# A hybrid retention and sparse-attention block: two projection chunks side by side, wider modulation sums, a re-cut last stage

## The reference, cut to what matters

```python
mod = silu(c) @ w_ada + b_ada                       # six vectors of 1024
sh1, sc1, ga1, sh2, sc2, ga2 = split(mod, 6)
h = rmsnorm(x, ln_mix_g) * (1 + sc1) + sh1
(rq, rk, rv, rg, nq, nkc, nvc, nks, nvs, nkw, nvw, ngate) = split(h @ w_in)   # 2840 columns
y_ret = retention(rope(rq), rope(rk) * RET_DK ** -0.5, rv) * silu(rg)
# three attention branches: compressed blocks, selected blocks, sliding window
y_nsa = nsa(rope(nq), nkc, nvc, rope(nks), nvs, rope(nkw), nvw, ngate, ...)
x = x + ga1 * (concat([y_ret, y_nsa]) @ w_out)
h2 = rmsnorm(x, ln_ffn_g) * (1 + sc2) + sh2
x = x + ga2 * ((silu(h2 @ w_ff_gate) * (h2 @ w_ff_up)) @ w_ff_down)
return rmsnorm(x, ln_final_g)
```

## Time and profile before

| | us |
|---|---|
| median of 3 runs | 727.98 |
| the profiled execution, device time | 729.54 |
| its span, first to last instruction | 727.70 |
| TensorE busy | 682.1 (94%) |
| VectorE busy | 332.8 (46%) |
| GpSimd busy | 265.9 (37%) |
| ScalarE busy | 225.5 (31%) |
| mean granted clock of TensorE | 0.976 of full |

### The profile page before, as it was taken

The page is one execution under the profiler, slowest core; times in us unless marked ns, Lnnn a source line. Parts: engine busy times, 40 slices in busy tenths (PEclk is TensorE's granted clock), DMA queues, the critical chain, the costliest instruction groups (busy, mean ns, idle before and its releaser), DMA issues.

```text
span 727.7 us, 9019 instructions
## 1 busy us (share of the span) xinstructions
PE 682.1 (94%) x3547; PEld 564.1 (78%) x3547; DVE 332.8 (46%) x587; ACT 225.5 (31%) x378; POOL 265.9 (37%) x127
## 2 busy tenths in 40 slices
PE   2678899999989898999999999999999999999995
PEld 1556679987768687888898888888888888888884
DVE  4878999977465668152620110000000029633126
ACT  4435233422132333332542222222222213232222
POOL 2316443432000111138034434434434427545531
PEclk9699999999998899999999999999999999999999
DMA  9975986665000000176014233233233223232002
GB/s 314 359 257 152 353 293 234 199 240 228 30 2 1 0 2 1 40 221 202 1 48 127 87 96 107 87 98 104 87 102 101 89 86 117 86 103 72 0 1 116
DMA packets 73962, 88.09 MB, mean 121 GB/s; under 512 B 3048, under 2 KB 57536, under 8 KB 73792
## 3 DMA queue, kind: packets, MB, share of 16 engines
q1 hardware_dynamic: 73184, 86.36, 36.0%
q0 software_dynamic: 416, 1.08, 0.4%
q10 hardware_dynamic: 320, 0.07, 0.0%
HBM read 85.41 MB, written 2.10 MB: 120 GB/s over the span
## 4 chain that ended last, share of the span: by engine, by line
PE 78%; DVE 10%; ACT 3%; issue 3%; DMA 3%; SPq 2%; POOL 0%; POOLq 0%; DVEq 0%
PE ps L1523 11%; PE ps L1524 11%; PE ps L1522 11%; PE ps L1141 11%; PE ps L1143 11%; PE ps L1142 11%; PE ps L1274 3%; DMA raw<-in_w_in 3%; DVE acc L732 2%; DVE ps L875 1%; SPq L344 1%; PE ps L1332 1%; PE ps L1399 1%; PE ps L1228 1%; ACT hf L488 1%
## 5 line engine op out<-in xcount | busy, mean ns | idle before, releaser
L404 POOL TENSOR_TENSOR wl<-raw,wh 128x1024 fp32r<-128x1024 f32 (+1 forms) x94 | 238.6, 2543 | 285.8 <-ACT wh L456 285.6
L456 ACT ACTIVATE wh<-raw 128x1024 fp32r<-128x1024 f32 (+1 forms) x94 | 97.4, 1039 | 154.4 <-PE ps L1524 73.9
L1522 PE MATMUL ps<-hTh,wh 128*128 128x512 f32 (+1 forms) x384 | 142.8, 372 | 0.0
L1523 PE MATMUL ps<-hTl,wh 128*128 128x512 f32 (+1 forms) x384 | 142.6, 371 | 0.0
L1524 PE MATMUL ps<-hTh,wl 128*128 128x512 f32 (+1 forms) x384 | 142.6, 371 | 0.0
L1106 DVE TENSOR_TENSOR act<-ps,sg 128x512 f32<-128x512 f32 x22 | 15.2, 692 | 212.3 <-PE ps L1524 212.3
L1141 PE MATMUL ps<-wh,hTh 128*128 128x512 f32 (+1 forms) x224 | 90.5, 404 | 11.8 <-DVE hTl L770 10.6
L1143 PE MATMUL ps<-wh,hTl 128*128 128x512 f32 (+1 forms) x224 | 85.8, 383 | 0.0
L1142 PE MATMUL ps<-wl,hTh 128*128 128x512 f32 (+1 forms) x224 | 85.7, 383 | 0.0
L1522 PEld LDWEIGHTS ps<-hTh,wh 128*128 128x128 f32 x384 | 72.4, 188 | 12.5
L1523 PEld LDWEIGHTS ps<-hTl,wh 128*128 128x128 f32 x384 | 72.4, 188 | 12.4
(11 more groups left out here) (197 smaller groups left out, 818.4 us busy)
## 6 DMA issues: line engine op xcount, KB each, us to landing
raw<-in_w_ada SPq DMA_DIRECT2D x32, 512.0 KB, 5.8
raw<-in_w_ff_gate SPq DMA_DIRECT2D x22, 512.0 KB, 3.8
raw<-in_w_ff_up SPq DMA_DIRECT2D x22, 512.0 KB, 3.7
raw<-in_w_ff_down SPq DMA_DIRECT2D x22, 512.0 KB, 3.2
raw<-in_w_in SPq DMA_DIRECT2D x20, 512.0 KB, 7.0
early<-in_w_ada SPq DMA_DIRECT2D x16, 512.0 KB, 9.6
raw<-in_w_out SPq DMA_DIRECT2D x8, 512.0 KB, 6.6
xs<-in_x SPq DMA_DIRECT2D x4, 512.0 KB, 5.3
```

The costliest lines, as they stand in the source:

```text
L404: pool.tensor_tensor(lo, raw[:, slot, 0:n], hi.bitcast(F32), ALU.subtract).then_inc(w_lo, 1)
L456: a.activation(split(u, n)[0], raw[:, slot, 0:n], ACT.Copy).then_inc(w_hi, 1)
L1522: mm(o, hi[:, ks], hTh[:, k, c0:c1], start=k == 0, stop=False)
L1523: mm(o, hi[:, ks], hTl[:, k, c0:c1], start=False, stop=False)
```

## The change

1. The chunks K_CMP and K_WIN run together: units 0, 2, 4, 6 are K_CMP's, units 1, 3, 5, 7 K_WIN's, both over the same quarter of the normed input. K_WIN's outputs lie in banks 4, 5 and 6 and, for the fourth tile, in two pieces in the free ends of banks 4 and 5. Its keys go through the same rotation as the selected keys (four heads at once).
2. ACT's `high` for the first units stands before the transposes' copies and after each pair of blocks, no longer between the two blocks of a pair. Evacuations, transposes, the MLP's waits and the sums for the later modulation vectors get new positions v.
3. `ada_early` treats the two modulation vectors in one instruction, 2 x 256 wide, eight instead of sixteen per quarter.
4. The ring carries five of the six vectors of w_ada until unit 21, the sixth (ga2) during the gate and up projections, where its two row sums follow `gate_up` 11 and 12. The load of the final norm's weights moves behind it.
5. Last stage: the last tile is cut in three pieces, the scaling by the norm's weights goes ahead of the power, DVE finishes one half of a tile and ACT the other, one tile later than before in the streams, and ACT issues the output DMA of its half.

```diff
...
-CHUNKS = [(C_CMP, 512), (C_Q, 512), (C_RQK, 512), (C_WIN, 280), (C_RG, 512), (C_RV, 512)]
-K_CMP, K_Q, K_RQK, K_WIN, K_RG, K_RV = range(6)
+CHUNKS = [(C_CMP, 512), (C_WIN, 280), (C_Q, 512), (C_RQK, 512), (C_RG, 512), (C_RV, 512)]
+K_CMP, K_WIN, K_Q, K_RQK, K_RG, K_RV = range(6)
...
+HALF = D // 2
+PIECES = [[(0, HALF), (HALF, D)]] * (TT - 1) + [[(0, HALF), (HALF, 768), (768, D)]]
...
-AHEAD = 4
+AHEAD = 2
...
-ADA_UNITS = 20
-ADA_OPS = 4 * ADA_START
+ADA_UNITS = 14
+ADA_LAST = 5 * KT
+ADA_FFN = U0_GU + 8
+ADA_OPS = 2 * ADA_START
...
+def chunk_of(u):
+
+    return (u % 2, u // 2) if u < 2 * UPC else divmod(u, UPC)
+
+
 def stream():
 
     items = []
     for q in range(UPC):
-        items += [("early", 4 * q + j) for j in range(4)] + [("w", q)]
+        items += [("early", 4 * q + j) for j in range(4)] + [("w", 2 * q), ("w", 2 * q + 1)]
     a = ADA_START
-    for u in range(3, UNITS):
-        if u > 3:
+    for u in range(2 * UPC - 1, UNITS):
+        if u >= 2 * UPC:
             items.append(("w", u))
-        upto = min(KT * len(ADA), ADA_START - (-(KT * len(ADA) - ADA_START) * (u - 2) // ADA_UNITS))
+        if u < ADA_FFN:
+            upto = min(ADA_LAST, ADA_START - (-(ADA_LAST - ADA_START) * (u - 2 * UPC + 1) // ADA_UNITS))
+        else:
+            upto = min(KT * len(ADA), ADA_LAST + (u - ADA_FFN) // 2 + 1)
         while a < upto:
             items.append(("ada", a))
             a += 1
...
+        def win_out(t):
+
+            if t < TT - 1:
+                return ps[:, 4 + t, 0:P], ps[:, 4 + t, P:280]
+            return ps[:, 4, 280:280 + P], ps[:, 5, 280:432]
...
-                    sp.wait_ge(roped, TT * (K_WIN + 1))
                     sp.dma_start(decay[:, :, :], decays).then_inc(decay_in, 16)
-                if (kind, j) == ("w", U0_GU - 1):
-
+                if (kind, j) == ("w", U0_GU + 34):
                     sp.wait_ge(mod_read, 10)
                     sp.dma_start(gfin[:, :], ln_final_g.partition_broadcast(P)).then_inc(gfin_in, 16)
+                if (kind, j) == ("w", U0_GU - 1):
+
...
-                sp.dma_start(out[t * P:(t + 1) * P, :], xb[:, t % 2, :]).then_inc(out_done[t], 16)
+                sp.dma_start(out[t * P:(t + 1) * P, 0:HALF], xb[:, t % 2, 0:HALF]).then_inc(out_done[t], 16)
             for t in range(TT):
-                sp.wait_ge(out_done[t], 16)
+                sp.wait_ge(out_done[t], 32)
...
-                if u == 3:
+                if u == 2 * UPC:
...
             high(0)
+            high(1)
...
             for k in range(KT):
-                if k % 2 and k < KT - 1:
-                    high(k // 2 + 1)
                 a.wait_ge(mod_read, k // 2 + 1)
...
                 a.activation(hTh[:, k, :], hf[:, k % 2, :], ACT.Copy).then_inc(h_hi, 1)
+                if k % 2 and k < KT - 1:
+                    high(k + 1)
+                    high(k + 2)
...
+                    if ch == K_WIN:
+                        a.wait_ge(unit_used, 2 * UPC)
...
+                    if ch in (K_Q, K_RQK):
+                        a.wait_ge(roped, TT * (ch - 2) + t + 1)
...
             for v in range(U_IN):
-                if v and v % UPC == 0:
-                    evacuate(v // UPC - 1)
-                if v and v + 3 < U_IN:
+                for ch in {7: [K_CMP], 8: [K_WIN], 12: [K_Q], 16: [K_RQK], 20: [K_RG]}.get(v, []):
+                    evacuate(ch)
+                if 2 * UPC <= v + 3 < U_IN:
                     high(v + 3)
-                if 5 <= v <= 8:
-                    pairs_copy(v - 5)
-                for n in {7: [0], 10: [1, 2], 12: [3, 4], 14: [5, 6], 16: [7, 8], 19: [9]}.get(v, []):
+                if 9 <= v <= 12:
+                    pairs_copy(v - 9)
+                for n in {11: [0, 1], 14: [2, 3], 15: [4, 5], 18: [6, 7], 19: [8, 9]}.get(v, []):
...
+            def finish(t):
+
+                a.wait_ge(y_scaled, piece_count(t, len(PIECES[t]) - 1))
+                a.wait_ge(rstd_ok, N_X2 + t)
+                a.activation(xb[:, t % 2, HALF:D], xb[:, t % 2, HALF:D], ACT.Copy, scale=rstd[:, t:t + 1]).then_inc(y_high, 1)
+                a.wait_ge(y_high, t + 1)
+                a.dma_start(out[t * P:(t + 1) * P, HALF:D], xb[:, t % 2, HALF:D]).then_inc(out_done[t], 16)
...
             for t in range(TT):
-                for half in range(2):
-                    a.wait_ge(x2_ok, 2 * t + half + 1)
-                    cols_ = slice(half * 512, (half + 1) * 512)
-                    if t >= 2 and half == 0:
-                        a.wait_ge(out_done[t - 2], 16)
-                    a.activation(xb[:, t % 2, cols_], x1[:, t, cols_], ACT.Square,
-                                 accum_out=(ssq, ssq2)[half][:, t:t + 1]).then_inc(sq3, 1)
+                for n, (c0, c1) in enumerate(PIECES[t]):
+                    a.wait_ge(x2_ok, piece_count(t, n))
+                    if t and n == 0:
+                        a.wait_ge(var_ok, N_X2 + t - 1)
+                    a.activation(sqj[:, c0 % HALF:c0 % HALF + c1 - c0], x1[:, t, c0:c1], ACT.Square, accum_out=part[:, n:n + 1]).then_inc(sq3, 1)
+                    if t and n == 0:
+                        finish(t - 1)
+            finish(TT - 1)
...
-                for o in ops:
-                    p, (kk, i) = 2 * q + o // 8, divmod(o % 8, 2)
-                    j, k = 2 * p + i, 4 * (p % 2) + kk
-                    d.wait_ge(early_in[j % EARLY], 16 * (j // EARLY + 1))
-                    dst = acc[:, i, 2 * q * P:2 * (q + 1) * P]
-                    src = early[:, j % EARLY, 2 * kk * P:2 * (kk + 1) * P]
+                for k in ops:
+                    kh, kk = divmod(k, 4)
+                    j = 4 * q + 2 * kh
+                    for i in range(2):
+                        d.wait_ge(early_in[(j + i) % EARLY], 16 * ((j + i) // EARLY + 1))
+                    dst = acc[:, :, 2 * q * P:2 * (q + 1) * P]
+                    src = early[:, j % EARLY:j % EARLY + 2, 2 * kk * P:2 * (kk + 1) * P]
                     if k == 0:
                         d.tensor_scalar(dst, src, cs[:, k:k + 1], None, ALU.mult).then_inc(ada_used, 1)
                     else:
-                        d.wait_ge(ada_used, 16 * q + o - 1)
+                        d.wait_ge(ada_used, KT * q + k)
                         d.scalar_tensor_tensor(dst, src, cs[:, k:k + 1], dst, ALU.mult, ALU.add).then_inc(ada_used, 1)
...
-            ada_early(0, range(16))
+            ada_early(0, range(KT))
...
                 if q < UPC - 1:
-                    ada_early(q + 1, range(AHEAD, AHEAD + 3))
+                    ada_early(q + 1, range(AHEAD, AHEAD + 2))
                 h_low(2 * q)
                 if q < UPC - 1:
-                    ada_early(q + 1, range(AHEAD + 3, AHEAD + 5))
+                    ada_early(q + 1, range(AHEAD + 2, AHEAD + 3))
                 h_low(2 * q + 1)
                 if q < UPC - 1:
-                    ada_early(q + 1, range(AHEAD + 5, 16))
+                    ada_early(q + 1, range(AHEAD + 3, KT))
...
-                for n in {7: [0], 10: [1, 2], 12: [3, 4], 19: [9]}.get(v, []):
+                for n in {11: [0, 1], 14: [2, 3], 15: [4, 5]}.get(v, []):
...
-                if v == 8:
+                if v == 11:
                     mod_rows(5, ga1, 0)
-                if v == 10:
+                if v == 12:
                     mod_rows(6, ga1, 1)
-                if v == 13:
+                if v == 17:
                     mod_columns(7, 2, 32, 0, KT, 48, 16).then_inc(mod_read, 1)
+                if v == 19:
+                    mod_columns(8, 3, 40, 0, KT, 40, None).then_inc(mod_read, 1)
...
-                if 4 <= v < UPC * (K_WIN + 1) + 2 and v % UPC < 2:
-                    rope_chunk(v // UPC - 1, (0, 1) if v % UPC == 0 else (2, 3))
-                if v == 17:
+                if 2 * UPC <= v < UPC * (K_RQK + 1) + 2 and v % UPC < 2:
+                    rope_chunk(v // UPC - 2, (0, 1) if v % UPC == 0 else (2, 3))
+                if v == 9:
                     d.wait_ge(proj_ev, TT * (K_WIN + 1))
                     d.tensor_scalar(gates[:, :, :], gates[:, :, :], 0.5, 0.5, ALU.mult, ALU.add).then_inc(gates_ok, 1)
                 if v == 18:
-                    mod_columns(8, 3, 40, 0, KT, 40, None).then_inc(mod_read, 1)
                     compressed()
...
+                if f == 12:
+                    mod_rows(9, ga2, 0, bank=4)
+                if f == 13:
+                    mod_rows(10, ga2, 1, bank=5)
                 for u in (U0_GU + 2 * f + 4, U0_GU + 2 * f + 5):
+                    for j in ada_after.get(u, []):
+                        ada(j)
...
+            def take(t, n):
+
+                c0, c1 = PIECES[t][n]
+                d.wait_ge(y_ps, 2 * t + c0 // HALF + 1)
+                d.tensor_tensor(x1[:, t, c0:c1], ps[:, 2 * t + c0 // HALF, c0 % HALF:c0 % HALF + c1 - c0], x1[:, t, c0:c1],
+                                ALU.add).then_inc(x2_ok, 1)
+
+            def scale_final(t, n):
+
+                c0, c1 = PIECES[t][n]
```

(79 more changed lines are left out.)

126 lines of the change are left out of this document (51 added, 75 removed).

## The result

The changed kernel takes 738.84 us (median of 4 runs, 738.15 to 739.73), the kernel before 727.43 us in the same measurement (4 runs, 725.49 to 729.76): ratio 1.0159, 95% interval 1.0129 to 1.0189. It is 1.6% slower; the forecast was 717.4 us and 1.5% faster. The profiled execution has a span of 736.3 us, against 727.70.

What follows compares the result with a forecast made beforehand. The prediction took TensorE, busy 94% of the span, as the bound, with DVE nearly a second bound from 60 to 161. Its six terms summed to -10.6 us, from the median 727.98 to 717.4 us; range 712.5 to 723.0.

Steps and rivals of the forecast that it cites:

- 1, K_WIN out of the dense stretch: TensorE's dense stretch: four K_WIN units of 3.16 us each, at full clock without a gap, leave it; -12.6 us.
- 2, K_Q's start: First stage: with K_WIN's units there, K_Q starts at 70.2 instead of 66.52; +3.7 us, bounds +1.5 to +9.
- 3, hole before the pair transposes: TensorE's 2.0 us wait before the pair transposes, behind a late load of w_in, goes; -2.0 us, ends 0 and -2.6.
- 4, lateness in the middle: After units 14 and 18, TensorE's waits for DVE move closer; 0 to 5 us lost, +1.0 taken.
- 5, wait for `ga`: Gate and up projections: TensorE stands still for two DVE instructions behind `gate_up` 12; +1.4 us, between 0.7 and 3.
- 6, end: Last tile: DVE no longer lags, and scaling is split between ACT and DVE; -2.1 us, between -3.4 and -1.0.
- The rival of a restart at the low clock: First stage's quarters: a late chain adds a restart at the low clock, about 1 us; within a rival of chance 0.17.
- the rule that the prediction cites: POOL and a DVE instruction with two SBUF inputs share a port lock; whoever issues first blocks the other throughout its instruction.
- The first rival: First stage: later quarters stay bound by DVE's chain as POOL's splits hold the port; 720 to 727, middle 722; chance 0.17.
- the warning sign named at the end: A hole of over 3 us on TensorE after units 14 or 18 would show the forecast wrong.
- The second rival: DVE, 93% busy there already, is the pace of the middle; lateness costs 5 instead of 1: 721.5 us; chance 0.15.

Runs made afterwards that it cites:

- e7: The kernel before with the new last stage alone (squares, power and scaling in pieces, output by halves from two queues): 725.12 us, ratio 0.9964.
- e5: The changed kernel with the early modulation sums 256 columns wide, 16 a quarter, as before the change: 736.64 us, ratio 1.0128.
- e4: The changed kernel with 18 matmuls of 512 columns, result not used, added on TensorE in the hole after unit 14: 731.48 us, ratio 1.0052.
- e9: The changed kernel with narrow (256-column) early sums for the first quarter alone, wide ones for the other three: 738.59 us, ratio 1.015.
- e12: The changed kernel with both late holes closed, narrow first-quarter sums, ga2 rows read before `act` 12, eight unused matmuls before the second column sums: 715.16 us.
- e6: The kernel before with the 512-wide early modulation sums alone: 729.92 us, ratio 1.002.
- e3: The changed kernel with DVE's late modulation sums redistributed among the units so that both holes, after units 14 and 18, close: 718.27 us, ratio 0.986.

## Why the prediction was wrong

The sum of the changed kernel, by its own steps, from the two profiled executions (736.3 - 727.7 = +8.6). Two of its parts have no counterpart in the forecast. Parts 1 and 3 stand with the forecast's size, since the matmuls and the wait are gone from where they stood; they were not measured by themselves, but the sum closes to 0.1 us with them.

| part | forecast | measured |
|---|---|---|
| 1, K_WIN out of the dense stretch | -12.6 | -12.6: no 280-column matmul after 73.80 |
| 2, K_Q's start | +3.7 | +7.3 (73.80 against 66.52) |
| 3, hole before the pair transposes | -2.0 | -2.0 |
| 4, lateness in the middle | +1.0 | idle time +8.0, low clock behind it +12.1 |
| 5, wait for `ga` | +1.4 | +1.45 |
| 6, end | -2.1 | -2.7; -3.0 alone (e7) |
| attention stage | 0 | -2.9, between executions, not of the change (see below) |
| sum | -10.6 | +8.6 |

**Part 4 is the step that failed, and it alone turned the sign.** The forecast named both places and found the two engines even there (20 to 22 us against 20.5), then took 1 us between 0 and 5. Two errors. The blocks were added up with mean durations, and not in DVE's order, where the two sums stand ahead of the rows that TensorE wants next; the holes were 4.0 and 4.0. And lateness was priced as idle time. The Q tiles' hole cost 13.0 and the other 7.1, since both runs of work behind them went at the low level of the clock, 1.2 GHz. The rival of a restart at the low clock was given "about 1" elsewhere; here it was 9.0 and 3.1 (and 1.5 for the first hole in the profile of e5). The Trainium skill, TensorE: Matmul & The Clock Gate, section HAM oscillation — how this bites in real kernels, warns that a long enough wait between bursts of matmuls lets the clock drop and the next burst begins cold. Trace and e4 agree: behind 4.0 us of standing still the clock is 0.50. The prediction had used to see this in the first stage and did not carry it to the middle.

**Part 2 failed at the start and at the second column sums.** The first matmul came at 29.85 against the 27.0 assumed, and the second sums at 36.34 against 32.3: 2.85 us of that are the start, the other 1.2 a wait for DVE (1.01 of it shown as idle time). In both places DVE's wide sums stand beside POOL's splits. DVE and POOL of the changed kernel in order of time, then single sums from the chain that ended last (start, us):

```profile
14.43 8.83 DVE L751 SCALAR_TENSOR_TENSOR acc<-early,cs,acc 128x512 f32<-128x512 f32 x7 [0.15 <-DVE acc L748]
18.17 4.54 POOL L425 TENSOR_TENSOR wl<-raw,wh 128x1024 fp32r<-128x1024 f32 x2 [4.84 <-ACT wh L477]
...
31.44 4.30 POOL L425 TENSOR_TENSOR wl<-raw,wh 128x1024 fp32r<-128x1024 f32 x2 [8.72 <-ACT wh L477]
```

```profile
17.97 0.76 DVE acc L751
18.85 2.64 DVE acc L751
21.62 1.65 DVE acc L751
...
31.87 2.65 DVE acc L751
```

Each sum waits for the one before, as all of them add to one accumulator, and POOL's two splits hold up one sum each: 2.64 and 1.65 us instead of 0.76. That agrees with the rule that the prediction cites from the Trainium skill, SBUF — State Buffer, section Who interferes with whom, and did not apply to the start. e5 and e9, with narrow sums there, start 2.1 and 2.5 us earlier. From the second column sums on the forecast held: sums at 36.34, 46.82 and 57.31, 10.5 us a quarter against 10.3. What the forecast missed is that an earlier start alone gives little or nothing (e9), because DVE has the second sums hardly sooner and the clock falls again; only with that hole filled (e12) does K_Q come at 71.7.

The first rival, a chain-bound quarter, came about in its mechanism and hardly in its price. POOL's splits do hold up the modulation's additions in every quarter (2.67 us at 42.30, 2.67 and 1.68 at 52.80 and 55.59), so that DVE needs not some 7 us a quarter, as forecast, but is busy 9.9 and 9.8 of the 10.5 us between column sums. TensorE's wait for it ahead of the sums is 1.2 us once and then 0.15 and 0.20. The wait for the low part is one of 2.9 at the very start.

**Parts 1, 3, 5 and 6 were right**, mechanism and size; so was the warning sign named at the end, "a hole after units 14 or 18 of over 3 us". With both holes closed, and nothing else mended, the kernel takes 718.3 us: the forecast of the rest was 717.4 with 1.0 for the middle. That it lies so near has luck in it: in its profile K_Q comes at 74.04 instead of 70.2, and the attention stage takes 2.9 us less than in the profile before, which no part foresaw.

The 2.9 us of the attention stage are the clock as well: from its landmark at 203.38 to that at 306.21 the kernel before reads a mean granted clock of 0.93, the changed one 0.97 over the same work (214.10 to 314.06, 99.96 us against 102.83). They do not belong to the change. The same stretch in e7_before_tail, whose code there is that of the kernel before:

```profile
204.72:305.18 100.46, 92.87 (x709) 76.16 (x708) 61.55 (x142) 33.41 (x82) 13.52 (x8) 0.97 0.00 1
```

In e6 it is 100.5 us as well, and in e5, with the changed kernel's code there, 102.8 at 0.93. So the stretch takes some 100 or some 103 us from execution to execution, whichever kernel it is in. An estimate from these rows: with 100.5 in the profile before, the sum would be +10.9 instead of +8.6, near the 11.4 us between the two medians. Why the clock differs there, no run shows.

The second rival (DVE as the pace of the middle, 721.5) had the right place and the wrong mechanism: DVE's order, not its load, made the holes, since e3 has the same load and no hole.

## What to carry to other kernels

Where a change moves waits closer together, write the slower engine's instructions down in their order up to each thing the dense engine waits for, and price each possible hole at itself plus the work behind it at the low clock; here 13.0 us for 4.0 of idle time. An ordering of filler work costs nothing to change and was worth 20 us. Where a hole can't be closed, useless matmuls in it can pay (e4, e12).
